# Modulation rows of several blocks summed up on one PSUM bank by row pairs, copied and turned once

## The reference

```python
mod_l = (silu(c)    @ w_mod[i] + b_mod[i])   # 6 x 1024 numbers, for the latent tokens
mod_c = (silu(c_ctx) @ w_mod[i] + b_mod[i])  # the same for the context tokens
sh1, sc1, gt1, sh2, sc2, gt2 = split(mod, 6)
h = rms_norm(x, g_norm_mix[i]) * (1 + sc1) + sh1;  x = x + gt1 * mixer(h)
h = rms_norm(x, g_norm_mlp[i]) * (1 + sc2) + sh2;  x = x + gt2 * square(relu(h @ w_in)) @ w_out
```

## Time and profile before

| what | us |
|---|---|
| median of 3 timed runs (range) | 3065.37 (3065.24 to 3071.54) |
| profiled execution | 3069.87 |
| its span | 3068.1 |
| TensorE busy | 2936.8 |
| VectorE busy | 1795.7 |
| ScalarE busy | 1192.2 |
| mean granted TensorE clock | 0.983 |

### The profile page before, as it was taken

How to read it: one execution, slowest core, us unless ns; L and a number is a source line. 1 busy time by engine, 2 the same in 40 slices (tenths; PEclk the granted TensorE clock), 3 DMA queues, 4 the chain that set the end, 5 groups by cost and what they waited for, 6 DMA issues and landing times.

```text
span 3068.1 us, 44248 instructions
## 1 busy us (share of the span) xinstructions
PE 2936.8 (96%) x18874; PEld 2407.6 (78%) x18874; DVE 1795.7 (59%) x2519; ACT 1192.2 (39%) x1674; POOL 303.3 (10%) x282
## 2 busy tenths in 40 slices
PE   8999989999999999999999999998999999998999
PEld 7988888997864788787667888875678888774899
DVE  4467766555456466654875666446646665546454
ACT  3245564435234422224244222344442223424443
POOL 1000001101000111112011000200121011000110
PEclk9999999999999999999999999999999999998999
DMA  7836324454310344433114444230044442211343
GB/s 283 315 129 241 128 80 165 165 180 167 124 53 28 124 178 153 149 124 126 68 42 165 160 156 159 89 142 28 15 165 151 158 158 98 104 61 42 137 180 124
DMA packets 59605, 407.57 MB, mean 133 GB/s; under 512 B 6504, under 2 KB 9832, under 8 KB 11024
## 3 DMA queue, kind: packets, MB, share of 16 engines
q1 hardware_dynamic: 58368, 401.03, 36.0%
q0 software_dynamic: 1040, 3.71, 0.4%
HBM read 403.62 MB, written 1.09 MB: 132 GB/s over the span
## 4 chain that ended last, share of the span: by engine, by line
PE 85%; DVE 8%; ACT 4%; issue 2%; POOL 0%; DMA 0%; DVEq 0%; ACTq 0%
PE bank L575 25%; PE bank L577 24%; PE bank L576 24%; DVE wlo L1934 3%; ACT whi L1304 2%; PE bank L1055 1%; PE bank L672 1%; PE bank L1105 1%; PE bank L1049 1%; PE bank L1180 1%; PE bank L1059 1%; PE bank L1196 1%; PE bank L1214 0%; ACT part L1561 0%; PE bank L681 0%
## 5 line engine op out<-in xcount | busy, mean ns | idle before, releaser
L1934 DVE TENSOR_TENSOR wlo<-raw,whi 128x2048 fp32r<-128x2048 f32 x282 | 649.3, 2303 | 437.4 <-ACT whi L1304 437.2
L1304 ACT CAST whi<-raw 128x2048 fp32r<-128x2048 f32 x282 | 536.7, 1903 | 630.5 <-PE bank L577 625.1
L575 PE MATMUL bank<-xnhi,whi 128*128 128x512 f32 (+1 forms) x1776 | 668.4, 376 | 28.3 <-DVE wlo L1934 13.0
L576 PE MATMUL bank<-xnlo,whi 128*128 128x512 f32 (+1 forms) x1776 | 653.4, 368 | 0.0
L577 PE MATMUL bank<-xnhi,wlo 128*128 128x512 f32 (+1 forms) x1776 | 653.2, 368 | 0.0
L575 PEld LDWEIGHTS bank<-xnhi,whi 128*128 128x128 f32 x1776 | 339.4, 191 | 125.7 <-issue 49.2
L577 PEld LDWEIGHTS bank<-xnhi,wlo 128*128 128x128 f32 x1776 | 340.0, 191 | 54.8
L576 PEld LDWEIGHTS bank<-xnlo,whi 128*128 128x128 f32 x1776 | 340.3, 192 | 50.9 <-issue 0.2
L575 PE MATMUL bank<-hidhi,whi 128*128 128x512 f32 (+1 forms) x1024 | 373.0, 364 | 0.0
L577 PE MATMUL bank<-hidhi,wlo 128*128 128x512 f32 (+1 forms) x1024 | 371.4, 363 | 0.0
L576 PE MATMUL bank<-hidlo,whi 128*128 128x512 f32 (+1 forms) x1024 | 371.3, 363 | 0.0
(11 more groups left out here) (327 smaller groups left out, 4191.0 us busy)
## 6 DMA issues: line engine op xcount, KB each, us to landing
raw<-in_wall SPq DMA_DIRECT2D x330, 1024.0 KB, 4.8
vraw<-in_wall SPq DMA_DIRECT2D x48, 1024.0 KB, 4.8
x<-in_x SPq DMA_DIRECT2D x2, 1024.0 KB, 7.2
bias<-relative_offsets POOLq DMA_DIRECT2D x2, 768.0 KB, 8.4
x<-relative_offsets POOLq DMA_DIRECT2D x2, 768.0 KB, 11.3
out<-x SPq DMA_DIRECT2D x1, 1024.0 KB, 4.8
vec<-in_vec SPq DMA_DIRECT2D x1, 665.0 KB, 9.6
cst<-in_cst SPq DMA_DIRECT2D x1, 467.0 KB, 10.8
```

The lines of the kernel that those rows point to most:

```text
L575: mm(out, wh, xh, start=first, stop=False)
L576: mm(out, wh, xl, start=False, stop=False)
L1304: nc.scalar.copy(b.whi[u % SPL][:], b.raw[pos % RAW][:]).then_inc(*R.made("hi_ready"))
L1934: ttn(b.wlo[u % SPL][:], b.raw[blocks[u] % RAW][:], b.whi[u % SPL][:], ALU.subtract).then_inc(*R.made("lo_ready"))
```

## The change

Several blocks now share one pair of copy and turn. `b.cond` has 10 more columns of zeros in front (`COND`), and a block takes a stretch of 32 columns that begins `2 * place` earlier than the vectors, so its sums fall on rows `2 * place` and `2 * place + 1` of each strip and zeros are added to the others. The blocks of one group go to bank 5 as one sum: only the first starts it and only the last stops it. Six blocks are together in layer 0, the four of a norm in the others. One copy and one turn with 12 or 8 moving columns follow. `mods`, `take_rows`, `take_mods` and `norm_mod` wait and count by groups.

The same is done with the groups of VectorE's blocks: `group_sums` uses as weights 32 columns with a single column of ones, at place `n`, and sums all four groups of a layer up in bank 6, with one row for each. One copy of the heads and one turn (16 moving columns instead of 4) follow in the unit in which the fourth group was turned. Constants `strips` goes, `one_row` comes, `heads` grows.

```diff
+VGROUPS = VMOD // VGROUP
+TOGETHER = 6
+COND = 2 * (TOGETHER - 1)
...
+def together(m):
+    first = MODU // TOGETHER
+    if m < MODU:
+        return m % TOGETHER, TOGETHER, m // TOGETHER
+    return (m - MODU) % GAPM, GAPM, first + (m - MODU) // GAPM
...
@@ mods
+            place, size, groups = together(m)
             if m > plain_blocks(layer) + first:
-                mod_sums(m - 1, layer, bank_of_sums, 0)
+                if place == 0:
+                    mod_sums(m - 1, layer, bank_of_sums)
...
-                last = mm(bank_of_sums[strip:strip + 32, 0:UC], b.cond[:, kk, :], w[:, kk, :],
-                          start=(kk < 4), stop=(kk >= 4))
+                last = mm(bank_of_sums[strip:strip + 32, 0:UC], b.cond[:, kk, COND - 2 * place:COND - 2 * place + 32],
+                          w[:, kk, :], start=(place == 0 and kk < 4), stop=(place == size - 1 and kk >= 4))
...
@@ mod_sums
-        pe.wait_ge(R.sems["mod_rows_taken"], m + 1)
+        pe.wait_ge(R.sems["mod_rows_taken"], groups + 1)
+        o = UC + 4 * (m - place - plain_blocks(layer))
+        out = bank_of_sums[:, o:o + 4 * size].rearrange("p (m c s) -> p m c s", c=2, s=2)
         for c in range(2):
-            o = UC + 4 * (m - plain_blocks(layer) - first) + 2 * c
-            last = mm(bank_of_sums[:, o:o + 2], b.modrow[:, c * P:(c + 1) * P], cst("strips"), start=True, stop=True)
+            last = mm(out[:, :, c, :], b.modrow[:, c * P:(c + 1) * P], cst("stripe")[:, 0:2 * size], start=True, stop=True)
...
@@ group_sums
-        pe.wait_ge(R.sems["group_rows"], done)
+        pe.wait_ge(R.sems["group_rows"], done // VGROUPS)
+        one = cst("one_row")[:, VGROUPS - 1 - n:VGROUPS - 1 - n + 32]
         for j in range(VGROUP):
-            last = mm(bank[6][32 * j:32 * j + 32, :], ones[:, 0:32], b.modacc[:, done % 2, j, :, :].rearrange("p a n -> p (a n)"),
-                      start=True, stop=True)
+            last = mm(bank[6][32 * j:32 * j + 32, :], one, b.modacc[:, done % 2, j, :, :].rearrange("p a n -> p (a n)"),
+                      start=(n == 0), stop=(n == VGROUPS - 1))
...
@@ stage
-            if layer < LAYERS - 1 and m >= VSTEP and m % VSTEP < 2:
-                (group_turn if m % VSTEP else group_sums)(m // VSTEP - 1)
+            if layer < LAYERS - 1 and m >= VSTEP and m % VSTEP == 0:
+                group_sums(m // VSTEP - 1)
+            if layer < LAYERS - 1 and m == VSPAN + 1:
+                group_turn()
...
@@ vectors: stage
-                take_rows(bank[5])
+                place, size, groups = together(plain_blocks(beside[0]) + beside[1])
+                if place == size - 1:
+                    take_rows(bank[5])
...
@@ multiply
-        if m > VSTEP and m % VSTEP == 1:
-            dve.wait_ge(*R.next("group_summed"))
+        if m == VSPAN + 1:
+            dve.wait_ge(*R.next("group_summed", VGROUPS))
             cp(b.heads[:], bank[6][:]).then_inc(*R.made("group_rows"))
...
@@ norm_mod
-        if ahead:
-            take_rows(bank[5])
...
-            if ahead and c in (1, 4):
-                take_rows(bank[5])
```

More of the change, by code:

```diff
@@ L79 @@
 CST, NCST = layout([("ident", P), ("ones", P), ("tri", P), ("blocks", P), ("causal", GCH), ("anticausal", GCH),
-                    ("restart", T2), ("strips", 2), ("stripe", 32), ("heads", 4)])
+                    ("restart", T2), ("stripe", 32), ("heads", 4 * VGROUPS), ("one_row", 31 + VGROUPS)])
 def constants():
@@ L98, in constants @@
     put("anticausal", (i[:, None] % GCH) >= j[None, :])
-    put("strips", i[:, None] % 32 == np.arange(2)[None, :])
     put("stripe", i[:, None] % 32 == np.arange(32)[None, :])
-    put("heads", i[:, None] == 32 * np.arange(4)[None, :])
+    j = np.arange(4 * VGROUPS)
+    put("heads", i[:, None] == 32 * (j % 4)[None, :] + j[None, :] // 4)
+    put("one_row", np.broadcast_to(np.arange(31 + VGROUPS) == VGROUPS - 1, (P, 31 + VGROUPS)))
     put("restart", np.broadcast_to(np.arange(T2) % GCH != 0, (P, T2)))
@@ L281, in mod_beside @@
     return None
+def together(m):
[3 more added lines that the diff above has]
+    return (m - MODU) % GAPM, GAPM, first + (m - MODU) // GAPM
+GROUP_ENDS = [m + 1 for m in range(MODU + 2 * GAPM * (LAYERS - 1)) if together(m)[0] == together(m)[1] - 1]
 def mod_first(layer, m):
@@ L671, in mods, with mod_sums @@
                 strip = 32 * (kk % 4)
-                last = mm(bank_of_sums[strip:strip + 32, 0:UC], b.cond[:, kk, :], w[:, kk, :],
-                          start=(kk < 4), stop=(kk >= 4))
+                last = mm(bank_of_sums[strip:strip + 32, 0:UC], b.cond[:, kk, COND - 2 * place:COND - 2 * place + 32],
+                          w[:, kk, :], start=(place == 0 and kk < 4), stop=(place == size - 1 and kk >= 4))
             last.then_inc(*R.made("mod_rows"))
             g["mods"] += 1
-    def mod_sums(m, layer, bank_of_sums, first):
-        pe.wait_ge(R.sems["mod_rows_taken"], m + 1)
+    def mod_sums(m, layer, bank_of_sums):
+        place, size, groups = together(m)
+        assert place == size - 1
+        pe.wait_ge(R.sems["mod_rows_taken"], groups + 1)
+        o = UC + 4 * (m - place - plain_blocks(layer))
+        out = bank_of_sums[:, o:o + 4 * size].rearrange("p (m c s) -> p m c s", c=2, s=2)
         for c in range(2):
-            o = UC + 4 * (m - plain_blocks(layer) - first) + 2 * c
-            last = mm(bank_of_sums[:, o:o + 2], b.modrow[:, c * P:(c + 1) * P], cst("strips"), start=True, stop=True)
+            last = mm(out[:, :, c, :], b.modrow[:, c * P:(c + 1) * P], cst("stripe")[:, 0:2 * size], start=True, stop=True)
         last.then_inc(*R.made("mod_ready"))
@@ L688, in group_sums, with group_turn @@
         pe.wait_ge(R.sems["mod_multiplied"], VGROUP * (done + 1))
[L689 removed]
+        pe.wait_ge(R.sems["group_rows"], done // VGROUPS)
+        one = cst("one_row")[:, VGROUPS - 1 - n:VGROUPS - 1 - n + 32]
         for j in range(VGROUP):
[L691 to L692 removed]
+            last = mm(bank[6][32 * j:32 * j + 32, :], one, b.modacc[:, done % 2, j, :, :].rearrange("p a n -> p (a n)"),
+                      start=(n == 0), stop=(n == VGROUPS - 1))
         last.then_inc(*R.made("group_summed"))
[L695 removed]
+    def group_turn():
         pe.wait_ge(*R.next("group_rows"))
         pe.wait_ge(*R.next("mod_taken"))
[L699 to L700 removed]
+        out = bank[5][:, UC:UC + 4 * VMOD].rearrange("p (a q s) -> p a q s", a=2 * VGROUPS, s=2)
         for q in range(VW // P):
@@ L1970, in take_rows @@
         m = g["rows"]
-        dve.wait_ge(R.sems["mod_rows"], m + 1)
+        dve.wait_ge(R.sems["mod_rows"], GROUP_ENDS[m])
         if m:
@@ L1977, in take_mods @@
     def take_mods(layer, k, n, sums):
-        dve.wait_ge(R.sems["mod_ready"], plain_blocks(layer) + k + n)
+        dve.wait_ge(R.sems["mod_ready"], together(plain_blocks(layer) + k + n - 1)[2] + 1)
         put_mods(layer, k, n, sums[:, UC + 4 * k:UC + 4 * (k + n)])
@@ L2008, in multiply @@
                     dve.wait_ge(R.sems["group_summed"], n // VGROUP - 1)
-            w, c = b.vraw[n % 2][:, 2 * kc:2 * kc + 2, :], b.cond[:, 4 * (block % 2) + kc, s:s + 1]
+            w, c = b.vraw[n % 2][:, 2 * kc:2 * kc + 2, :], b.cond[:, 4 * (block % 2) + kc, COND + s:COND + s + 1]
             acc = b.modacc[:, n // VGROUP % 2, 2 * (block // 2 % 2) + s, :, :]
@@ L2017, in multiply @@
             ins.then_inc(*R.made("mod_multiplied" if op % 8 == 7 else "dve_step"))
-        if m > VSTEP and m % VSTEP == 1:
-            dve.wait_ge(*R.next("group_summed"))
+        if m == VSPAN + 1:
+            dve.wait_ge(*R.next("group_summed", VGROUPS))
             cp(b.heads[:], bank[6][:]).then_inc(*R.made("group_rows"))
-        if m > VSTEP and m % VSTEP == 2:
-            group = m // VSTEP - 1
+        if m == VSPAN + 2:
             dve.wait_ge(*R.next("group_ready"))
-            o = UC + 4 * VGROUP * group
-            put_mods(layer, 2 * GAPM + VGROUP * group, VGROUP, bank[5][:, o:o + 4 * VGROUP])
+            put_mods(layer, 2 * GAPM, VMOD, bank[5][:, UC:UC + 4 * VMOD])
     def take_to(buf, t, off=0, reverse=False, scale=None):
```

8 lines of the change are left out of this document (4 added, 4 removed).

## The result

| | before | after |
|---|---|---|
| median of the timed runs, us (range, runs) | 3065.37 (3064.93 to 3071.54, 5) | 3043.39 (3038.15 to 3050.98, 5) |
| profiled execution, us | 3069.87 | 3048.77 |
| its span, us | 3068.1 | 3047.0 |
| mean granted clock | 0.983 | 0.983 |

The ratio is 0.9925 with a 95% interval of 0.9904 to 0.9946: 22 us faster, with an interval of 17 to 29 us. The forecast was 3046 us.

A forecast was written before the change was run, and what follows sets the result against it. The prediction took TensorE's queue to bound the kernel. Its terms, 7.0 + 10.5 + 2.9 - 0.2 - 1.0 = 19.2 us, taken off the median of 3065.4 us gave 3046.2 us, with a range of 3038 to 3056 us.

The forecast's parts named there:

- What bounds the kernel: Whole kernel: TensorE, busy 2936.8 of 3068.1 us, sets the time; instructions off its queue save their slots where it never pauses.
- Term 1: Layer 0, beside the projections: 20 turns of row blocks go at 0.35 us each, 7.0 us saved.
- Term 2: MLPs: nine turns of row groups go, six at 1.30 us and three at 0.90 us, 10.5 us saved.
- Term 3: Six norms with blocks: 0.35 us at each fourth block, 0.8 us at the first norm, 2.9 us saved.
- Term 4: Turns that stay, in blocks and MLPs: more moving columns make them cost 0.2 us more.
- Term 5: TensorE's clock behind norms: merged pauses may drop it in four, costing 2.1 us; another gives 1.1 us back; net 1.0 us lost.
- the step that the sum is complete: Whole kernel: the terms make up all 19.2 us; wider constants only add 18 KB to a starting load, at nothing.
- A: Layer 0: the weight stream sets the pace, so the 7.0 us for row turns is lost; 3053.2 us, chance 0.06.
- E: Whole change: it doesn't do what it says, copies or turns stay as many; 3065 us, chance 0.01.
- B: Four norms: the clock falls in all for the 6.8 us stretch, costing 13.6 us; 3058.8 us, chance 0.05.
- D: Six norms: merged pauses drop the clock for 10.3 us each, making the kernel slower; 3072.7 us, chance 0.02.
- C: Removed turns: small matmuls are worth nothing, switching cost stays, only waits are saved; 3062.8 us, chance 0.03.

The follow-up runs named there:

- e7: The changed kernel with the conditioning vectors' buffer ahead of the weights', making the distance of weights and columns a multiple of 256 bytes; 3052.64 us, ratio 0.9952 to before.
- e1: The kernel before with unused SBUF columns so every buffer lies where the changed kernel has it, no instruction different; 3056.73 us, ratio 0.9975.
- e6: The kernel before with 64 unused bytes a partition between the split weights and the columns they multiply; 3055.95 us, ratio 0.9965.
- e4: The changed kernel with one more filler matmul behind the third block of each of the six norms; 3042.87 us, ratio 0.9917 to before.
- e11: The changed kernel with one `mod` buffer (384 bytes) moved ahead of `raw`, so all distances are 192 over a multiple of 256; 3068.80 us, ratio 1.0000 to before.
- e12: The changed kernel with a filler matmul in the norms and buffers moved to distance 192 in the first model, 0 in the second; 3033.99 us, ratio 0.9895 to before.

## Why the prediction was right, and where it wasn't

**What bounds the kernel: right.** TensorE's queue has no slack in the dense stages, so slots taken off it are time.

**Term 1 (7.0 us): right in the trace.** 0.55 to 0.21 us is 0.34 us a turn, 6.8 us for 20; between before and e7, at equal spacing, 6.9 us. At distance 64 some of it is lost again between the turns: fewer products go at the faster of the two speeds in the kernel after than in e1 (117.6 against 117.2 ns over 2,895 products, 114.9 against 113.4 ns over 329 with tokens out), about 1.7 us.

**Term 2 (10.5 us): right.** Against e1, which has the same distance, the starts move by 1.26, 1.25 and 0.91 us at the three turns of a layer, 10.3 us in three layers; between before and e7 by 10.8 us. A turn that waited was read at 1.30 us, between the two; in e1 it takes 1.70 us (1163.36 to 1165.06) where it took 1.76 before.

**Term 3 (2.9 us): right.** 0.33 us at each of the six fourth blocks, 0.85 us at the first norm (e1 to after), nothing ahead of the first product in the norm read above, whose 6.31 us didn't move.

**Term 4 (0.2 us): no step of this size is seen.** The kept turn with 12 columns takes the same slot of some 0.44 us. (The constants grow by 45 columns, 23 KB, not 18 KB; 18 KB is `one_row` alone.)

**Term 5 (1.0 us): right in kind, half in size.** Two of four norms fell. Against e1 the starts move back by 0.9 us at each of the two and by 0.3 us at the norm at 1617 us, 2.1 us. The cost of the four was well put: the prediction's four chances in ten at 1.3 us against 13 in 24 at 0.9 us is 2.1 against 2.0 us. What failed is the 1.1 us that the norm at 1632 us was to give back: it gave none.

**What failed is the step that the sum is complete.** "Go at nothing" was said of the wider constants as a load at the start. Their bytes, and those of `cond`, move every later buffer, and that is worth 7.7 us by e1's ratio, 10.7 us by e6's and 8 to 9 us by e7 against the kernel after. No row of before shows it, since it shows only one distance.

On the other side the direct terms stand in the medians as 13.3 us (after against e1) and 14.5 us (e7 against before), less than the 19.2 us of the forecast. In the traces they are there. Before to e7 the profiled executions differ by 19.5 us, as read above. From e1 to after the removed turns move the starts by 20.0 us, but these two executions differ by only 8.5 us. Of the 11.4 us that are lost between the turns, 1.7 us are the slower products of term 1, 2.1 us the norms of term 5, 1.1 us lie in the first 25 us, and some 6 us in narrow work of the last layer, two steps of 3 us where the clock was low in the execution of after and not in that of e1. The first of them, after and then e1, in windows over the same work:

```profile
2751.50:2760.00 8.50, 7.60 (x32) 3.51 (x32) 3.14 (x9) 0.59 (x1) 0.00 (x0) 0.62 0.01 2
2766.00:2773.00 7.00, 5.97 (x42) 3.32 (x40) 4.12 (x12) 0.59 (x1) 0.00 (x0) 1.00 0.00 0
```

Such stretches differ from one execution to the next, and the filler kernel e4, with nothing changed there, gets 9.7 us back behind 2600 us against this execution. Whether the change makes them more frequent isn't shown; so 3 to 5 us between the terms and the medians stay open. The two errors, some 8 us too little and some 5 us too much, nearly cancelled, and that is luck: it is why 3046 us was close to 3043 us.

**Rivals.** A and E are out by the rows above. B and D: no norm of the kernel after fell for more than 3.4 us that had not fallen before, and two of four stayed up; over six kernels 13 of 24 fell, and where the starts were lined up (after, e7) a fall cost 0.9 us, against the 3.4 us that B needs. C is out: the blocks follow directly, at 0.21 us. (Its 0.30 us for a wait is 0.40 us by term 2's own rows, 1.76 less 1.36 us; that moves it by 0.6 us and changes nothing.)

## What to carry to other kernels

Small matmuls with full weights in the queue of the engine that sets the time cost their whole slot (0.34 us for four passes with two columns each), and accumulating before one common turn gives that slot back in the trace; the medians showed 13 to 15 us of the 19 to 20 us here. When an edit changes the size of any buffer, compare the distance of the starts of equal products in both traces before giving the time to the edit, and time the old kernel with the new places. If TensorE is the bound, the distance between the buffers of its two operands is worth a few tries: here the same instructions, only with buffers moved, took 3052.6 us at 0 and 3076.4 us at 128.

## What the runs showed of the hardware

The distance in SBUF between the weights and the moving columns of fp32r products changes the distance of their starts at full clock, by up to 5% with 256 columns (113 to 120 ns) and 3% with 512 (226.8 to 233.4 ns). 0 is the best of the five values tried with 512 columns and the worst with 256, 192 nearly the reverse. The order isn't that of the size of the distance, but the sign counts: with the roles of the operands swapped, 64 behaves as 192 does and 192 as 64. At 64 and 192 single units go at 113 or at 118 ns, and how many go fast differs between kernels of one distance, so the distance isn't all of it. Moving both by the same 192 bytes changes nothing. Why the distance matters is not measured. Only multiples of 32 bytes were tried. That 256 is a period is borne out by three pairs: 66,816 and 65,792 bytes (before, e7), 67,136 and 66,880 bytes (e1, e6), and for 256 columns 66,752 and 65,984 bytes (e11, e12) behave alike, while 0, 64, 128 and 192 all differ. Beyond these values it isn't shown. The Trainium skill (TensorE: Matmul & The Clock Gate, "Step-by-step: what each phase is for") says that the weight load and the moving operand have separate read ports and that loading doesn't take bandwidth from the running matmul; these runs don't measure ports, but the two operands are not independent of each other in where they lie.

The clock of TensorE held over a norm with one pause of 2.12 us that ends at 1033 us and fell behind pauses of the same form that end at 1402 and 1989 us, so one trace of such a norm doesn't tell what the next will do. Over the kernels of this study it fell in 13 of 24 such norms, in 1 of 20 where the narrow turn split the pause into 0.42 and 0.76 us, and in none of 12 with a filler that left a pause of 1.06 us.
